# Two transformer stacks on one NeuronCore: another place for the shared buffer, predicated copies in a recurrence, and new orders of steps

## The reference

```python
for l in range(2):
    x = x + gate1 * token_mixing(x, ...)     # four branches, gated and merged:
    #   differential attention (4 heads), latent attention (8 heads),
    #   short convolution (3 taps), long convolution (31 taps) + layernorm
    x = x + gate2 * channel_mixing(x, ...)   # up, 3-tap convolution, silu, down
```

```python
h = x + 0.5 * swiglu(rmsnorm_2(x, g[0]), w_ffn_gu[layer, 0], w_ffn_down[layer, 0])
h = h + mix(rmsnorm_2(h, g[1]))
h = h + 0.5 * swiglu(rmsnorm_2(h, g[2]), w_ffn_gu[layer, 1], w_ffn_down[layer, 1])
x = h + sigmoid(rmsnorm_2(h, g[3]) @ w_ple_gate[layer]) * (p[layer] @ w_ple_proj[layer])
```

```python
decay = jnp.exp(jnp.where(causal[:, :, None], b[t] - b[s], -jnp.inf))
A = jnp.einsum('bhtk,bhsk,bhtsk->bhts', q_, k_, decay)
o_intra = jnp.einsum('bhts,bhsv->bhtv', A, v_)
```

## Time and profile before

| | us |
|---|---|
| median of 3 runs | 3467.45 (3466.78 to 3470.16) |
| profiled execution | 3468.48 |
| its span | 3466.7 |
| TensorE busy in it | 3254.7 |
| VectorE busy | 2475.9 |
| ScalarE busy | 1762.6 |

### The profile page before, as it was taken

How to read it: one execution, slowest core, us unless ns; L and a number is a source line. 1 busy time by engine, 2 the same in 40 slices (tenths; PEclk the granted TensorE clock), 3 DMA queues, 4 the chain that set the end, 5 groups by cost and what they waited for, 6 DMA issues and landing times.

```text
span 3466.7 us, 64588 instructions
## 1 busy us (share of the span) xinstructions
PE 3254.7 (94%) x27162; PEld 3153.1 (91%) x27162; DVE 2475.9 (71%) x3728; ACT 1762.6 (51%) x2673; POOL 3.0 (0%) x6
## 2 busy tenths in 40 slices
PE   6899899999999999979999998999999999998998
PEld 6789899988989899879999978999989999987998
DVE  8987798887667766876575666667576667688665
ACT  4555444455454545664454445455455455457444
POOL 0000000000000000000000000000000000000000
PEclk8899999989999999989999999999999999998999
DMA  8445487434546455425545433554533554542453
GB/s 304 144 170 200 163 308 286 151 125 140 177 158 225 158 184 183 153 74 198 187 166 186 174 122 131 188 183 171 184 133 137 183 183 171 188 165 87 161 186 112
DMA packets 163920, 597.93 MB, mean 172 GB/s; under 512 B 18192, under 2 KB 18224, under 8 KB 163376
## 3 DMA queue, kind: packets, MB, share of 16 engines
q1 hardware_dynamic: 163632, 593.81, 48.8%
HBM read 592.69 MB, written 1.05 MB: 171 GB/s over the span
## 4 chain that ended last, share of the span: by engine, by line
PE 80%; DVE 14%; ACT 4%; issue 2%; DMA 1%; SPq 0%; DVEq 0%; ACTq 0%
PE ps L451 25%; PE ps L452 25%; PE ps L453 25%; DVE wlo L415 4%; DVE fa L1520 1%; ACT whi L403 1%; PE ps L1112 1%; DVE hl L1737 1%; DVE land L526 0%; PE ps L654 0%; PE ps L1228 0%; DVE tmps L559 0%; DMA land<-w_ada 0%; DMA land<-w_in 0%; DVE tmps L557 0%
## 5 line engine op out<-in xcount | busy, mean ns | idle before, releaser
L451 PE MATMUL ps<-hh,whi 128*128 128x256 f32 x5472 | 1547.5, 283 | 59.5 <-DVE hl L1737 27.2
L452 PE MATMUL ps<-hl,whi 128*128 128x256 f32 x5472 | 1539.6, 281 | 0.0
L453 PE MATMUL ps<-hh,wlo 128*128 128x256 f32 x5472 | 1535.2, 281 | 0.0
L415 DVE TENSOR_TENSOR wlo<-land,whi 128x1024 fp32r<-128x1024 f32 (+1 forms) x1032 | 1217.5, 1216 | 224.1 <-ACT whi L403 223.3
L403 ACT ACTIVATE whi<-land 128x1024 fp32r<-128x1024 f32 (+1 forms) x1032 | 1028.2, 1044 | 171.8 <-PE ps L453 157.2
L451 PEld LDWEIGHTS ps<-hh,whi 128*128 128x128 f32 x5472 | 1037.5, 190 | 67.9 <-issue 50.4
L452 PEld LDWEIGHTS ps<-hl,whi 128*128 128x128 f32 x5472 | 1037.6, 190 | 0.6
L453 PEld LDWEIGHTS ps<-hh,wlo 128*128 128x128 f32 x5472 | 1037.5, 190 | 0.0
L451 PE MATMUL ps<-ra,whi 128*128 128x256 f32 (+1 forms) x2416 | 691.0, 286 | 20.9 <-DVE ra L1428 10.4
L453 PE MATMUL ps<-ra,wlo 128*128 128x256 f32 (+1 forms) x2416 | 688.0, 285 | 0.0
L452 PE MATMUL ps<-ra,whi 128*128 128x256 f32 (+1 forms) x2416 | 686.9, 284 | 0.0
(11 more groups left out here) (415 smaller groups left out, 2427.4 us busy)
## 6 DMA issues: line engine op xcount, KB each, us to landing
land<-w_gu SPq DMA_DIRECT2D x352, 512.0 KB, 3.5
land<-w_dn SPq DMA_DIRECT2D x176, 512.0 KB, 3.6
land<-w_in SPq DMA_DIRECT2D x136, 512.0 KB, 3.5
land<-w_ada SPq DMA_DIRECT2D x96, 512.0 KB, 3.8
land<-w_up SPq DMA_DIRECT2D x88, 512.0 KB, 4.1
land<-hg_in SPq DMA_DIRECT2D x64, 512.0 KB, 3.5
land<-w_down SPq DMA_DIRECT2D x44, 512.0 KB, 4.5
land<-ple_gate SPq DMA_DIRECT2D x32, 512.0 KB, 3.5
```

The source lines that it names most:

```text
L415: dve.tensor_tensor(w.lo, g.slot(n), w.hi.bitcast(F32), ALU.subtract).then_inc(*D_("w_lo", n))
L451: pe.matmul(out, w.hi, x.hi, start=first, stop=False, skip_group_check=skip)
L452: pe.matmul(out, w.hi, x.lo, start=False, stop=False, skip_group_check=skip)
L453: return pe.matmul(out, w.lo, x.hi, start=False, stop=last, skip_group_check=skip)
```

## The change

1. ra1, fa1 and crow are allocated right behind x, hh and hl, with ra2 and fa2 in the same place; par and all that follows it come behind them. No size changes.
2. In the HGRN stages, levels 2 to 6 are no longer masked into tmps and added to A32. One copy_predicated writes the level's values from PSUM into A32 where the mask is set, after the preceding level is in. ScalarE's diagonal step waits for that in place of the sum.
3. MIX_ORDER and HGRN_ORDER list the same steps in another order.

```diff
@@ Program.__init__
         self.h = Pair(self.hh, self.hl)
+        with ExitStack() as inner:
+            self.ra1 = inner.enter_context(nc.sbuf_tensor("ra1", [128, 6656], F32R))
+            self.fa1 = inner.enter_context(nc.sbuf_tensor("fa1", [128, 11392], F32))
+            self.crow = inner.enter_context(nc.sbuf_tensor("crow", [128, TILE], F32))
+        self.ra2 = sb("ra2", 4096, F32R)
+        self.fa2 = sb("fa2", 15104)
         self.par = sb("par", NPAR)
...
-        with ExitStack() as inner:
-            self.ra1 = inner.enter_context(nc.sbuf_tensor("ra1", [128, 6656], F32R))
-            self.fa1 = inner.enter_context(nc.sbuf_tensor("fa1", [128, 11392], F32))
-            self.crow = inner.enter_context(nc.sbuf_tensor("crow", [128, TILE], F32))
-        with ExitStack() as inner:
-            self.ra2 = inner.enter_context(nc.sbuf_tensor("ra2", [128, 4096], F32R))
-            self.fa2 = inner.enter_context(nc.sbuf_tensor("fa2", [128, 15104], F32))
@@ MIX_ORDER
-    norm:0 cf:0 cf:1 lam:0 conv:0 conv:1 cf:2 cf:3 qk:0 conv:2 conv:3 conv:4 scu:0 qk:1 conv:5 conv:6 scu:1 conv:7
-    qk:2 qk:3 conv:8 mla:0 conv:9 mla:1 tables:0 conv:10 v:0 v:1 conv:11 conv:12 tables:1 da_scores:0 conv:13
-    conv:14 da_combine:0 conv:15 mc:0 da_scores:1 conv:16 mla_square:0 da_combine:1 da_turn:0 da_scores:2 mla_norm:0
-    conv:17 da_values:0 conv:18 da_combine:2 da_turn:1 da_scores:3 mla_apply:0 da_combine:3 mla_square:1 scu:2
-    da_values:1 da_turn:2 scu:3 da_values:2 da_turn:3 uq:0 ya_square:0 mla_norm:1 sc_conv:0 conv:19 sc_conv:1
-    da_values:3 scb:0 sc_conv:2 sc_conv:3 ya_square:1 scb:1 gate2:0 gate2:1 wo2:0 merge2:0 wo2:1 mla_apply:1
-    ya_norm:0 merge2:1 wo2:2 gate2:2 merge2:2 gate2:3 wo2:3 uq:1 ya_apply:0 merge2:3 uq:2 ya_norm:1 rope:0 rope:1
-    ya_apply:1 rope:2 uq:3 rope:3 rope:4 kr_all:0 ukv:0 ukv:1 ukv:2 cf_sum:0 mv:0 ukv:3 mv:1 mla_scores:0 gate1:0
+    norm:0 cf:0 cf:1 lam:0 conv:0 cf:2 conv:1 qk:0 conv:2 cf:3 conv:3 qk:1 conv:4 conv:5 scu:0 conv:6 conv:7 qk:2
+    conv:8 scu:1 conv:9 qk:3 mla:0 v:0 tables:0 conv:10 mla:1 conv:11 v:1 mc:0 conv:12 tables:1 conv:13 mla_square:0
+    da_scores:0 conv:14 da_combine:0 mla_norm:0 conv:15 da_scores:1 conv:16 da_combine:1 da_turn:0 da_scores:2
+    da_values:0 conv:17 da_combine:2 da_turn:1 da_scores:3 mla_apply:0 da_combine:3 mla_square:1 scu:2 da_turn:2
+    scu:3 da_turn:3 da_values:1 uq:0 mla_norm:1 conv:18 da_values:2 sc_conv:0 sc_conv:1 scb:0 sc_conv:2 da_values:3
+    sc_conv:3 scb:1 gate2:0 gate2:1 wo2:0 ya_square:0 wo2:1 ya_square:1 mla_apply:1 ya_norm:0 merge2:0 merge2:1
+    gate2:2 gate2:3 wo2:2 wo2:3 merge2:2 uq:1 ya_apply:0 merge2:3 uq:2 ya_norm:1 rope:0 rope:1 ya_apply:1 rope:2
+    uq:3 rope:3 rope:4 kr_all:0 conv:19 cf_sum:0 ukv:0 ukv:1 ukv:2 mv:0 ukv:3 mv:1 mla_scores:0 gate1:0 mla_scale:0
...
@@ HGRN_ORDER
-    norm:0.0 q:0.0 token:0.0 q:0.1 q_out:0.0 q_out:0.1 f:0.0 f_out:0.0 f:0.1 v:0.0 f_out:0.1 f:1.0 v:0.1 prepare:0.0
-    token_columns:0.0 v_out:0.0 q:1.0 cross64:0.0 q:1.1 level:0.0 level:0.1 level:0.2 q_out:1.0 level:0.3 q_out:1.1
-    level:0.4 f_out:1.0 v:1.0 f:1.1 level:0.5 f_out:1.1 level:0.6 v:1.1 cross128:0.0 diagonal:0.0 prepare:1.0
-    v_out:1.0 gate:0.0 gate:0.1 values:0.0 cross64:1.0 sum:0.0 sum:0.1 cross128:1.0 level:1.0 level:1.1 factor:0.0
-    level:1.2 gate_out:0.0 gate_out:0.1 level:1.3 finish:0.0 level:1.4 gate:0.2 level:1.5 level:1.6 gate:0.3
+    norm:0.0 q:0.0 token:0.0 q_out:0.0 q:0.1 f:0.0 q_out:0.1 f_out:0.0 f:0.1 q:1.0 f_out:0.1 f:1.0 q:1.1 v:0.0
+    prepare:0.0 cross64:0.0 v:0.1 level:0.0 level:0.1 level:0.2 q_out:1.0 level:0.3 token_columns:0.0 q_out:1.1
+    v_out:0.0 level:0.4 f_out:1.0 f:1.1 level:0.5 f_out:1.1 v:1.0 cross128:0.0 level:0.6 v:1.1 diagonal:0.0
+    prepare:1.0 v_out:1.0 gate:0.0 gate:0.1 values:0.0 cross64:1.0 sum:0.0 sum:0.1 factor:0.0 cross128:1.0 level:1.0
+    level:1.1 level:1.2 gate_out:0.0 gate_out:0.1 level:1.3 finish:0.0 level:1.4 gate:0.2 level:1.5 level:1.6
...
@@ hgrn_scalar, step diagonal
-            act.wait_ge(*W("A32", st, gr, 6))
+            act.wait_ge(*W("level_out", st, gr, 6))
@@ hgrn_vector, step level (i > 1)
-            a = g.t(6 + i % 2)[:, 0:256]
-            dve.tensor_tensor(a.rearrange("p (n t) -> p n t", t=32), src, mask, ALU.mult).then_inc(
+            dve.wait_ge(*W("level_out", st, gr, i - 1))
+            dve.copy_predicated(M.A32.rearrange("p (n t) -> p n t", t=32),
+                                mask.bitcast(U32).unsqueeze(1).broadcast_to([128, 8, 32]), src).then_inc(
                 *D_("level_out", st, gr, i))
-            dve.wait_ge(*W("level_out", st, gr, i))
-            dve.tensor_tensor(M.A32, M.A32, a, ALU.add).then_inc(*D_("A32", st, gr, i))
-            dve.wait_ge(*W("A32", st, gr, i))
```

More of the change, by code:

```diff
@@ L9 @@
 F32R = mybir.dt.float32r
+U32 = mybir.dt.uint32
 I32 = mybir.dt.int32
@@ L214, in tensor_reduce, with copy_predicated @@
         return self
+    def copy_predicated(self, *a, **k):
+        return self
     def tensor_copy(self, *a, **k):
@@ L977 @@
-    da_values:3 scb:0 sc_conv:2 sc_conv:3 ya_square:1 scb:1 gate2:0 gate2:1 wo2:0 merge2:0 wo2:1 mla_apply:1
-    ya_norm:0 merge2:1 wo2:2 gate2:2 merge2:2 gate2:3 wo2:3 uq:1 ya_apply:0 merge2:3 uq:2 ya_norm:1 rope:0 rope:1
-    ya_apply:1 rope:2 uq:3 rope:3 rope:4 kr_all:0 ukv:0 ukv:1 ukv:2 cf_sum:0 mv:0 ukv:3 mv:1 mla_scores:0 gate1:0
-    mla_scale:0 cf_mean:0 mla_scores:1 mla_turn:0 mla_scale:1 mla_scores:2 gate1:1 mla_turn:1 mla_scale:2
-    mla_values:0 mla_scores:3 cf_square:0 gate1:2 mla_values:1 cf_norm:0 mla_turn:2 mla_scores:4 cf_apply:0
@@ new lines @@
+    gate2:2 gate2:3 wo2:2 wo2:3 merge2:2 uq:1 ya_apply:0 merge2:3 uq:2 ya_norm:1 rope:0 rope:1 ya_apply:1 rope:2
+    uq:3 rope:3 rope:4 kr_all:0 conv:19 cf_sum:0 ukv:0 ukv:1 ukv:2 mv:0 ukv:3 mv:1 mla_scores:0 gate1:0 mla_scale:0
+    mla_scores:1 mla_scale:1 mla_scores:2 mla_scale:2 cf_mean:0 mla_turn:0 gate1:1 mla_scores:3 cf_square:0
+    mla_turn:1 gate1:2 mla_values:0 mla_values:1 mla_turn:2 cf_norm:0 mla_scale:3 cf_apply:0 mla_scores:4 gate1:3
+    mla_scores:5 mla_turn:3 wo0:0 mla_scale:4 gate0:0 mla_scale:5 cf_silu:0 mla_values:2 mla_values:3 merge0:0
@@ L987 @@
+    gate0:1 mla_scores:6 mla_scores:7 mla_scale:6 cf_apply:1 mla_turn:4 gate0:2 wo0:1 merge0:1 mla_turn:5 wo0:2
+    mla_values:4 mla_values:5 mla_turn:6 gate0:3 cf_silu:1 merge0:2 wo0:3 mla_values:6 mla_scale:7 gate3:0 merge0:3
+    gate3:1 wo3:0 merge3:0 mla_turn:7 wo3:1 wo3:2 gate3:2 merge3:1 merge3:2 mla_values:7 wo3:3 gate3:3 merge3:3
+    wo1:0 wo1:1 wo1:2 wo1:3 merge1:0 merge1:1 merge1:2 merge1:3 out:0 out:1 out:2 out:3 end:0
 """
@@ L1878 @@
 HGRN_ORDER = """
-    norm:0.0 q:0.0 token:0.0 q:0.1 q_out:0.0 q_out:0.1 f:0.0 f_out:0.0 f:0.1 v:0.0 f_out:0.1 f:1.0 v:0.1 prepare:0.0
-    token_columns:0.0 v_out:0.0 q:1.0 cross64:0.0 q:1.1 level:0.0 level:0.1 level:0.2 q_out:1.0 level:0.3 q_out:1.1
-    level:0.4 f_out:1.0 v:1.0 f:1.1 level:0.5 f_out:1.1 level:0.6 v:1.1 cross128:0.0 diagonal:0.0 prepare:1.0
-    v_out:1.0 gate:0.0 gate:0.1 values:0.0 cross64:1.0 sum:0.0 sum:0.1 cross128:1.0 level:1.0 level:1.1 factor:0.0
-    level:1.2 gate_out:0.0 gate_out:0.1 level:1.3 finish:0.0 level:1.4 gate:0.2 level:1.5 level:1.6 gate:0.3
-    diagonal:1.0 gate_out:0.2 values:1.0 finish:0.1 sum:1.2 sum:1.3 factor:1.0 gate_out:0.3 finish:1.2 finish:1.3
-    end:0.0
+    norm:0.0 q:0.0 token:0.0 q_out:0.0 q:0.1 f:0.0 q_out:0.1 f_out:0.0 f:0.1 q:1.0 f_out:0.1 f:1.0 q:1.1 v:0.0
[3 more added lines that the diff above has]
+    level:1.1 level:1.2 gate_out:0.0 gate_out:0.1 level:1.3 finish:0.0 level:1.4 gate:0.2 level:1.5 level:1.6
+    gate:0.3 diagonal:1.0 gate_out:0.2 values:1.0 finish:0.1 sum:1.2 sum:1.3 factor:1.0 gate_out:0.3 finish:1.2
+    finish:1.3 end:0.0
 """
@@ L2301, in hgrn_vector @@
                 continue
-            mask = g.C("lev", (i - 1) * 32, 32).unsqueeze(1).broadcast_to([128, 8, 32])
+            mask = g.C("lev", (i - 1) * 32, 32)
             src = g.ps[3 + i % 2][:, 0:256].rearrange("p (n t) -> p n t", t=32)
@@ L2307, in hgrn_vector @@
                     dve.wait_ge(*W("diagonal", st, 0))
-                dve.tensor_tensor(M.A32.rearrange("p (n t) -> p n t", t=32), src, mask, ALU.mult).then_inc(
-                    *D_("level_out", st, gr, 1))
+                dve.tensor_tensor(M.A32.rearrange("p (n t) -> p n t", t=32), src,
+                                  mask.unsqueeze(1).broadcast_to([128, 8, 32]), ALU.mult).then_inc(*D_("level_out", st, gr, 1))
                 continue
-            a = g.t(6 + i % 2)[:, 0:256]
-            dve.tensor_tensor(a.rearrange("p (n t) -> p n t", t=32), src, mask, ALU.mult).then_inc(
+            dve.wait_ge(*W("level_out", st, gr, i - 1))
+            dve.copy_predicated(M.A32.rearrange("p (n t) -> p n t", t=32),
+                                mask.bitcast(U32).unsqueeze(1).broadcast_to([128, 8, 32]), src).then_inc(
                 *D_("level_out", st, gr, i))
-            dve.wait_ge(*W("level_out", st, gr, i))
```

(2 more changed lines are left out.)

## The result

The changed kernel takes 3444.26 us (median of 6 runs, 3442.15 to 3458.87), the kernel before 3468.92 (6 runs beside it): ratio 0.9936, 95% interval 0.9919 to 0.9952, 24.7 us less. The prediction was 3445.5. The profiled execution took 3443.94, its span is 3442.1.

The account below looks back on a forecast made before the run. TensorE, busy 94% of the span, bounds the kernel; savings of 15.9 (move), 3.9 (HGRN stages) and 2.2 (mixing) sum to 22.0 us, from 3467.45 to 3445.5 us. Range 3439 to 3452, chance 0.64; eight in ten 3430 to 3462.

Parts of the forecast that it names:

- step 1: Union buffer moved to hh's offset: 7248 ra matmuls go from 120.0 to 117.8 ns, 15.9 us less; bounds 0 and 23.
- rival A: The union buffer's place does not matter, ra's matmuls stay at 120.0 ns; time 3461.4 us; chance 0.18.
- Step 2: HGRN levels 2 to 6: twenty predicated copies replace multiply-add pairs, 9.2 us less VectorE; stages 1.2 and 1.7 us shorter.
- low end: Each predicated copy takes as long as the masked multiply it replaces (417 ns), saving the add's 0.46 us.
- cover: HGRN head group 1: VectorE comes 2.3 us earlier, but TensorE gains only 0.4 (first stage) or 0.9 (other).
- Step 3: New HGRN order: nothing in layer 0; in layer 3 level 2 on comes 1.0 us sooner despite a new 1.7 wait.
- Step 4: New mixing order: 0 for the differential attention scores, 1.1 us less per layer at rope, 2.2 us together.
- The walk: Differential attention scores, TensorE from v:1 to scu:2: waits move ahead but their sum stays; 0 in both layers.
- my bound of 154.5: First mixing stage: late end of the range 152.1 to 154.5 for the walk's end at scu:2, 153.3 before.
- The rope part: Mixing stages: gap of 1.77 us goes to 0.7, the 5.22 before rope 3 stays; 1.1 us less per layer.
- B: Rival: clock stays at 2.4 GHz through both layers' scores, or ra gains 3.2 ns; time 3430 us; chance 0.12.
- C: Rival: place matters but the new addresses clash more, 9.8 us slower, time 3477.3 us; chance 0.06.

Follow-up runs that it names:

- e1: The kernel before with only the union buffer moved behind hl, old orders and multiply-add pairs kept: 3441.24 us, ratio 0.9921.
- e4: The kernel before with the union buffer still at the back but 320 bytes lower, ra 32 above a multiple of 1024: 3446.14 us, ratio 0.9932.
- e2: The changed kernel without the move: union buffer last in the partition, new orders and predicated copies kept: 3466.05 us, ratio 0.9990.
- e5: The changed kernel with weight buffers put 32 above a multiple of 1024, hh staying at 32 and ra going to 64: 3488.42 us, ratio 1.0052.
- e9: The changed kernel with the mixing order of the kernel before: 3444.30 us, ratio 0.9924.
- e10: The changed kernel with the HGRN order of the kernel before: 3441.46 us, ratio 0.9919.
- e11: The changed kernel with the twenty predicated copies turned back into a masked multiply and an add each: 3454.33 us, ratio 0.9962.
- e12: The changed kernel with the old mixing order and x, hh, hl, ra 16 instead of 32 above a multiple of 1024: 3441.81 us, ratio 0.9920.
- e6: The changed kernel with x, hh, hl at 16 above a multiple of 1024 and ra at 64: 3465.44 us, ratio 0.9985.
- e3: The changed kernel without the 32-byte pad ahead of x, so x, hh, hl and ra lie at whole multiples of 1024: 3503.36 us, ratio 1.0098.

## Why the prediction was right, and where it was not

The time came out within 1.3 us, but not by its terms: step 1 was too small by some 12 us, steps 2 to 4 together too large by some 3 (without the move) to 9 (with it), by medians whose intervals are several us wide. That the two errors cancel is luck. Within steps 2 to 4 the copies gave more than forecast, and the new orders lengthened the two stages in which they changed something clearly (the first mixing stage, the first HGRN stage).

**Step 1 (15.9 predicted, 27.7 measured by e1, interval 21.5 to 33).** The mechanism holds: 352 was the bad place, hh's offset the good one, and rival A is refuted by e1 and e4 (ra shorter wherever it lies at 32) with e2 (long again at 352). One correction: I spoke of where the operand lies, and by e5 it is how it lies against the weight buffers. The size failed in the target that I took. I read 117.8 off one stretch of hh matmuls and made it what offset 32 gives. It is one of two levels. ra fell to 116.7, so 7248 x 3.2 = 23 us, the bound that I had drawn from the group means. And hh and hl, costed at nothing, fell too: in the kernel before they ran at 117.8 to 117.9 in six of the eight blocks and at 116.7 in two, which other stretches of its trace show. In such a block this is 1056 x 1.1 = 1.2 us, beside ra's 528 x 3.3 = 1.7; the block shown first loses 2.8, where I had 1.2. Counted over the profiles with these offsets, hh and hl are at the lower level in 46 of 56 blocks where ra lies at 16 or 32 as they do (changed kernel 7, e1 8, e4 4, e9 6, e10 6, e11 7, e12 8), in 4 of 16 where ra lies at 352 (the kernel before, e2), and in 5 of 8 where it lies at 64 (e6). The kernel before and e2 run the same instructions at the same addresses in these blocks, yet the fourth and seventh are at the lower level in one, the third and seventh in the other: addresses alone don't pick it. Why ra's place shifts hh's share, and what picks the level, stays open.
The Trainium skill gives TensorE's moving operand and its weight loads two read ports that are independent of each other ("SBUF — State Buffer", Who interferes with whom), and a matmul a time by its columns alone ("VectorE: DVE Perf Modes", the TRN2 errata). Against the changed kernel's 116.7 ns, e5 and e3 show 119.9 and 120.0 for the same instruction by 32 bytes of distance to the weights, so for these matmuls an address counts as well.

**Step 2 (2.9 predicted).** The copy was sized well. The twenty of them, count and min/median/max ns:
```profile
L2315 DVE COPY_PREDICATED fa<-con,ps x20: 431/440/454, 1437.4 to 3170.2; 128x256 f32<-128x256 uint32 x20
```
That is near the low end, the masked multiply's 417. The gap before level 4 is 2.32 in e10 and 2.90 in e1, 0.6 shorter, as forecast. What failed is the cover behind it, which I had at 0.4 and 0.9 us: e11 puts the copies' worth at 2.9 and 4.5 us in the two stages, where I had 1.2 and 1.7. By the windows above, 1.9 of the first stage's 2.9 is TensorE's busy time (149.77 against 147.91), with more of it at half clock (41.1 us at the 1.2 GHz level in e11, 30.7 in the changed kernel). In the last stage its busy time is the same (149.71 and 149.82) and the stage has 34.2 us at half clock in e11, 37.6 in the changed kernel: there all of it is time in which TensorE waits, 32.5 us against 27.9.

**Step 3 (1.0 gained in layer 3 and nothing in layer 0 predicted; by e10 2.3 lost in layer 0, nothing shown in layer 3).** Timeline of the changed kernel, last HGRN stage, behind the new wait:
```profile
3084.28 1.94 PE L1973 MATMUL ps<-fa 128*64 128x64 f32 x16 [2.65 <-DVE fa L2286]
...
3086.15 0.80 PE L454 MATMUL ps<-whi,hh 128*128 128x512 f32 x1
...
3093.98 0.66 PE L1997 MATMUL ps<-fa 128*32 128x32 f32 x29
...
3098.03 1.08 PE L1997 MATMUL ps<-fa 128*32 128x32 f32 x64 [2.78 <-DVE fa L2177]
```
The wait stands where I put it, before cross64 (L1973), and TensorE comes to it when I said (3081.6, 45.5 after the stage's start). It lasts 2.65, not 1.7, as VectorE brings K's product 0.9 later than in my walk. The gap before level 1 is gone. But behind the wait the granted clock is 0.50:
```profile
3084.00:3090.70 6.70, 6.42 (x27) 5.38 (x28) 5.76 (x9) 3.58 (x6) 0.00 (x0) 0.50 0.07 24
```
v:0.1, from 3086.15 to 3093.98, takes 7.8 us instead of 5.9, and level 2 comes 61.9 us after the stage's start, where it came at 59.1. I had it 1.0 sooner. e9 runs the same steps with 3.4 us at half clock behind this wait instead of 6.9; there level 2 comes at 60.7, and the stage is the 1.2 us shorter. Even so it is later than in the old order. In layer 0 the same wait (1.40 long) appears, where I had no change.

**Step 4 (2.2 gained predicted; 2.5 lost in the first layer, 0 in the second).** TensorE in the first mixing stage after:
```profile
133.58 0.80 PE L1087 MATMUL ps<-tmps,con 128*128 128x256 f32 x1 [5.55 <-DVE tmps L1546]
...
135.26 0.79 PE L1115 MATMUL ps<-fa 64*128 64x128 f32 x2 [0.46 <-ACT attn L1240]
...
143.87 0.79 PE L1115 MATMUL ps<-fa 64*128 64x128 f32 x2 [2.53 <-ACT attn L1240]
...
156.49 0.52 PE L454 MATMUL ps<-hh,whi 128*128 128x256 f32 x1
...
229.76 1.07 PE L1163 MATMUL ps<-fa,con 96*96 96x256 f32 x4 [1.40 <-DVE tmps L1480]
...
238.18 2.88 PE L1163 MATMUL ps<-fa,con 96*96 96x256 f32 x6 [5.25 <-ACT fa L1372]
```
The gap of 5.6 at mla_norm is there as forecast. The walk failed at "the waits move ahead, their sum stays". The waits from v:1 to scu:2 even sum to less (8.5 us for 9.8 in the first layer, 4.5 for 5.7 in the second), but moved ahead they put more matmuls at half clock: scores 1, 2 and 3 take 5.2 us each, and scu:2, at 156.5, begins 37.2 after v:1's end where it began 35.3 after, past my bound of 154.5 even with v:1's end 1.3 later. It runs at half clock too, 8.2 us for 5.7. In the second layer scu:2 comes at 735.7, v:1 0.4 later than before; my bound was 734.4, so this is past it too. The rope part holds there: the gap of 1.77 is 0.37 and the 5.22 keeps its length. In the first layer 1.5 goes from the one (2.92 before, 1.40 now) and comes back at the other (3.70 before, 5.25 now), no gain. The test that I set, a mixing stage 3 us longer, is met against e1's 381.2 alone, not against the mean of the old order. What refutes step 4 in the first layer is that each of the three stages with the new order and ra at 32 (384.6 to 384.9) is longer than each of the four with the old one (381.2 to 383.5), where it had 1.1 less.

**The rivals.** B happened by half: ra's 3.2 ns came, the full clock in the scores did not, the opposite did. C's clash doesn't happen, and no offset tried puts ra's matmuls above 120.0 ns. But e3 shows that a new place can cost more than C had, 59 us, when it takes hh and hl to 120.0 as well.

## What to carry to other kernels

Where matmuls run back to back, read ns per matmul off the starts of several stretches, by operand buffer and by stage: a difference between buffers of one shape may be an address, as here, and 32 bytes of pad between the weights and the moving operand were worth 59 us of 3503 here. Behind gaps of 1.5 to 5.6 us in the scores TensorE's work ran at half clock, so that a gap cost more than its length there; when an order moves waits, add up what stands behind each, not the waits alone. And a right total proves no term: the move alone (e1) and all but the move (e2) split it in two runs.

## What the runs showed of the hardware that was not expected

- A 128x256 float32 matmul in a dense stream, with new weights loaded for each, takes 116.7 to 120.0 ns by how its moving operand lies against the weight buffers (the table). Of the nine distances tried, 16 and 32 bytes are best, 0, 64 and 352 worst; 128 as a modulus doesn't fit. With no DMA and no split under way the difference is the same (120.0 in e3, 116.7 in the changed kernel).
- At a distance of 16 or 32 bytes there are two levels, 116.7 and 117.8 to 117.9 ns. Each of the eight feed-forward blocks of the second stack stays at one of them from end to end, and which one differs from block to block. Such a block is 1.7 us longer or shorter by it (189.7 and 188.0 in e9 and the changed kernel). In the first stack the level can change within a stage: in the profile after, hh's groups go from 116.7 to 117.8 at 490.1, where a group of ra begins with one step of 0.16 us; other groups begin so without a change of level.
- copy_predicated from PSUM under a broadcast mask takes 440 ns for 128x256, 23 more than the multiply by the same mask.
